# A tenth slot for expert weights, and four units of them asked for earlier, in a two-layer mixer and mixture-of-experts kernel

## The chip, the core and the metric

The kernel runs on one core of a Trainium2 chip. The metric is the device time in microseconds of one execution; the figure given for a kernel is the median of its runs.

## The reference

Two layers over x of 256 tokens by 2048, all float32. Each layer:

```
z   = h @ w_in[l]                       # 2048 x 5648, split into 13 parts
mix = concat(rg_lru(..), short_conv(..), gla(..), local_attention(..)) @ w_out[l]
h   = layer_norm(ALPHA * h + mix)
g   = top-1 of 4 groups of softmax(h @ w_rg + b_rg);  e = top-2 of its 4 experts
ffn = sum over the chosen experts of weight * (silu(h @ w_gate[e]) * (h @ w_up[e])) @ w_down[e]
h   = layer_norm(ALPHA * h + ffn)
```

There are 16 experts per layer; w_gate[e] and w_up[e] are 2048 x 512, w_down[e] is 512 x 2048, so an expert's weights are 12 MB and a layer's 192 MB. All of them are read, once per layer.

## The kernel before

Five engines run hand-ordered streams and meet at semaphores. SyncE issues almost every load, on one queue.

*Projections.* The input projection (11 column blocks of 512) and the output projection (4) are cut into 60 quarters of 1 MB, numbered n. `load_quarter` (L333) puts quarter n into one of six raw buffers (`w_raw(n % 6)`, 8 KiB per partition each, at the start of `room`), and for n of 6 or more waits until TensorE is done with quarter n-6 (`w_used`, L345: at least n - 5). ScalarE rounds a quarter to fp32r (`round_w`, L522 to L527) when TensorE is done with quarter n-4, VectorE subtracts to get the rest (`split_w`, L1143), and TensorE multiplies three times (L815, L818, and L975 in the output projection). Between the quarters stand the pieces of the four mixers: the LRU's product (`lru_done`), the rounding and splitting of the mix (`mix_rounded`, `mix_split`).

*Experts.* An expert's weights are six units of 2 MB: four of gate and up (`unit_gu`), two of down (`unit_down`). They go into nine slots in turn, unit u into slot u % 9, at the places of `SLOT_KIB` in `room`, which the projections used before. Unit u has two DMAs of 1 MB each (L439 for gate and up, L443 for down). In SyncE's loop over the 96 units of a layer, units 0 to 2 follow quarter 59 at once, unit 3 waits for quarter 56 of the output projection (`NQ - 4`), units 4 and 5 for 58, unit 6 for 60; at unit 9 (`u == SLOTS`) SyncE also asks for the norm's gain and shift (L414, L416), and from there unit u waits until the last block of tokens of its slot's former expert has used it: after each quarter of the gate and up product (`gu_quarter`, `gu_done`), after half the down product (`y_half`) or after all of it (`y_done`).

*Order of experts.* The tokens are sorted into blocks of 32 per expert. Experts 0 and 1 always come first (`FIXED = 2`), the others by their number of blocks, most first. Their numbers are in a table that VectorE writes (L1638 and the tensor_tensor after it, `tab_ready`); SyncE waits for it at unit 12, the first of the third expert. Ahead of it in VectorE's order stand the multiply of h by the gain (after `gb1_loaded`), `hidden` of the first block and the second half of that multiply.

*Blocks.* `expert_block` (TensorE) multiplies a block by gate and up (L1080), gathers the next block's rows (L1022), adds the former block's result into h (L1037), transposes (L1089, L1030), and does the down product in two halves (L1098). Experts run in a hardware loop: its body holds three experts, it turns five times, and the sixteenth expert stands behind it. Inside it each expert has a loop over its blocks.

*The next layer.* `load_entry` (L348) asks for quarters 0 and 1 of the next layer when the last block's gate and up product is done (`gu_done`), for 2 to 5 when its down product is (`y_done`). ScalarE rounds quarter 0 ahead of its part of the final layer norm (L750 to L754).

The memory for GpSimd's DMA descriptors has its default size before; GpSimd issues no DMA in this kernel.

Of the kernel before, what the change touches and what calls it, by code (L numbers as in the profile page):

```python
# [15 lines left out]
P = 128  # L16
BLK = 32
KB = 256
# [28 lines left out]
def trunk(nc, x, ln0_g, ln0_b, w_in, conv_a_w, conv_a_b, lru_wa, lru_ba, lru_wx, lru_bx, lru_lam, conv_b_w,  # L47
          gla_wa2, gla_ba2, gla_norm_w, att_rel_bias, w_out, ln1_g, ln1_b, w_rg, b_rg, w_re, b_re,
          w_gate, w_up, w_down, ln2_g, ln2_b, out):
    _, T, D = x.shape  # L50
    L, E = w_gate.shape[0], w_gate.shape[1]
# [11 lines left out]
    NQ = 4 * (N_IN + N_OUT)  # L63
    UNITS = 6
    AHEAD = 3
    SLOTS = 9
    PER_E = 6
    FIXED = 2
    assert NQ % UNITS == 0 and T == 256 and D == 2048 and F == 512
    ALPHA = float((2 * L) ** 0.25)  # L70
    LN_EPS, RMS_EPS = 1e-5, 1e-6
# [3 lines left out]
    with ctx:  # L75
        def sb(name, shape, dt=F32):
            return ctx.enter_context(nc.sbuf_tensor(name, shape, dt))
# [9 lines left out]

        room_at = (nc.sbuf_base + 31) // 32 * 32
        room = sb("room", [P, 184 * KB])
        ring_at, arena_at = room_at, room_at + 96 * 1024  # L90
        SLOT_KIB = (64, 80, 112, 0, 16, 128, 32, 48, 96)

        def part(name, shape, at):

# [131 lines left out]
            return room[:, i * 2048:i * 2048 + 2048].rearrange("p (k n) -> p k n", k=4)  # L226

        def slot_words(u):
            at = SLOT_KIB[u % SLOTS] * KB
            return room[:, at:at + 4096]  # L230

        def unit_gu(u):

            return slot_words(u).rearrange("p (m k n) -> p m k n", m=2, k=4)

        def unit_down(u):

            return slot_words(u).rearrange("p (f n) -> p f n", f=2)
# [72 lines left out]
        def expert_row(eng, row, e):  # L311


            lo, hi = {0: (1, T // BLK), 1: (0, 4096), 2: (0, E - 1), 3: (1, 4096), 4: (E, NB_MAX), 5: (E - 1, 4096)}[row]
            return eng.value_load(tabi[0:1, row, bass.ds(e, 1)], min_val=lo, max_val=hi)
# [17 lines left out]
        def _(eng):  # L333
# [13 lines left out]
            def load_entry(l):  # L347

                if l:
                    last_block = expert_row(eng, 3, E - 1)  # L350
                    eng.wait_ge(gu_done, last_block)
                for n in range(2):
                    load_quarter(l, n)
                if l:
                    eng.wait_ge(y_done, last_block)
                for n in range(2, UNITS):
                    load_quarter(l, n)
                if l == 0:
                    for v in range(2 * L):
                        for m in range(2):  # L360
                            src = ((ln1_g, ln1_b), (ln2_g, ln2_b))[v % 2][m][v // 2]
                            eng.dma_start(lnc[:, v + 1, m, :], src.rearrange("(p k) -> p k", k=KD)).then_inc(lnc_loaded, 16)
                    for m in range(1, L):
                        load_parameters(eng, m)
                eng.wait_ge(pads_ready, l + 1)
                for c in range(4):
                    eng.dma_start(c_wa2[32 * c:32 * c + RANK, :], gla_wa2[l]).then_inc(small_loaded.sem, 16)
                eng.dma_start(c_wca[:, :, 0:RANK], w_in[l, :, C_A:C_A + RANK].rearrange("(p k) n -> p k n", k=KD)
                              ).then_inc(small_loaded.sem, 16)
                load_vectors(*((ln0_g, ln0_b) if l == 0 else (ln2_g[l - 1], ln2_b[l - 1])))  # L370

            def load_vectors(g, b):
                for m, v in enumerate((g, b)):
                    eng.dma_start(gb_in[:, m, :], v.rearrange("(o n) -> o n", o=1).to_broadcast([P, D])
                                  ).then_inc(gb_in_loaded, 16)
# [6 lines left out]
            for l in range(L):  # L382
                for m, w in enumerate((lru_wa, lru_wx)):
                    eng.dma_start(r_w[:, m, :, :], w[l].rearrange("h i j -> i h j")).then_inc(lru_loaded.sem, 16)
                for n in range(UNITS, 18):
                    load_quarter(l, n)
                eng.wait_ge(gsc_done.sem, gsc_done.at(l, 1))
                rb = att_rel_bias[l]
                src = bass.AP(tensor=rb.tensor, offset=rb.offset + P + 1,
                              ap=[[1, P], [att_rel_bias.shape[2], HEADS], [1, T]])  # L390
                eng.dma_start(blocks(a_H, HEADS), src).then_inc(bias_loaded.sem, 16)
                for n in range(18, 40):
                    load_quarter(l, n)
                eng.wait_ge(att_pT.sem, att_pT.at(l, 1))
                eng.dma_start(wr[:, :, 0:G], w_rg[l].rearrange("(p k) g -> p k g", k=KD)).then_inc(router_loaded.sem, 16)
                eng.dma_start(wr[:, :, G:NR], w_re[l].rearrange("(p k) g -> p k g", k=KD)).then_inc(router_loaded.sem, 16)
                eng.dma_start(br[:, 0:G], b_rg[l:l + 1].to_broadcast([P, G])).then_inc(router_loaded.sem, 16)
                eng.dma_start(br[:, G:NR], b_re[l:l + 1].to_broadcast([P, E])).then_inc(router_loaded.sem, 16)
                for n in range(40, NQ):
                    load_quarter(l, n)  # L400

                eng.wait_ge(mix_split.sem, mix_split.at(l, 4))

                def weights(w, e):

                    if e < FIXED:
                        return w[l, e]
                    return w.rearrange("l e a b -> (l e) a b")[bass.ds(l * E + number, 1)].rearrange("o a b -> (o a) b")

                for u in range(PER_E * E):  # L410
                    e, i = u // PER_E, u % PER_E
                    if u == SLOTS:
                        eng.wait_ge(rows_zero.sem, rows_zero.at(l, 1))
                        eng.dma_start(gain_1, ln1_g[l:l + 1].to_broadcast([P, D])).then_inc(gb1_loaded.sem, 16)  # L414

                        eng.dma_start(shift_rows[0:P:BLK, :], ln1_b[l].rearrange("(c n) -> c n", c=4)).then_inc(gb1_loaded.sem, 16)  # L416
                    if e == FIXED and i == 0:
                        eng.wait_ge(tab_ready.sem, tab_ready.at(l, 1))
                    if e >= FIXED and i == 0:
                        number = expert_row(eng, 2, e)  # L420
                    if u >= SLOTS:

                        if u == SLOTS:
                            eng.wait_ge(tab_first.sem, tab_first.at(l, 1))
                        if u == SLOTS or (u - SLOTS) % PER_E == 0:
                            last_block = expert_row(eng, 3, (u - SLOTS) // PER_E)
                        eng.wait_ge((*gu_quarter, gu_done, y_half, y_done)[(u - SLOTS) % PER_E], last_block)
                    elif u == 2:
                        eng.wait_ge(w_used.sem, w_used.at(l, 4 * N_IN))
                    elif u == 3:  # L430
                        eng.wait_ge(w_used.sem, w_used.at(l, NQ - 4))
                    elif u == 4:
                        eng.wait_ge(w_used.sem, w_used.at(l, NQ - 2))
                    elif u == 6:
                        eng.wait_ge(w_used.sem, w_used.at(l, NQ))
                    if i < 4:
                        for m, w in enumerate((w_gate, w_up)):
                            src = weights(w, e).rearrange("(p k) n -> p k n", k=KD)
                            eng.dma_start(unit_gu(u)[:, m], src[:, 4 * i:4 * i + 4, :]).then_inc(unit_loaded[u % SLOTS], 16)  # L439
                    else:  # L440
                        src = weights(w_down, e).rearrange("(k p) n -> p k n", p=P)
                        for f in range(2):
                            eng.dma_start(unit_down(u)[:, f, :], src[:, 2 * (i - 4) + f, :]  # L443
                                          ).then_inc(unit_loaded[u % SLOTS], 16)
                if l + 1 < L:
                    load_entry(l + 1)
                else:
                    eng.wait_ge(y_done, expert_row(eng, 3, E - 1))
                    load_vectors(ln2_g[l], ln2_b[l])
# [313 lines left out]
        def _(eng):  # L763
# [31 lines left out]
            for l in range(L):  # L795
# [270 lines left out]
                def expert_block(g, first_unit, period):  # L1066

                    def loaded(u):
                        per_layer = len(range(u % SLOTS, PER_E * E, SLOTS))
                        eng.wait_ge(unit_loaded[u % SLOTS], period * 64 + 32 * (per_layer * l + u // SLOTS + 1))  # L1070

                    eng.wait_ge(xe_ready, g + 1)
                    for i in range(4):
# [43 lines left out]
                    with eng.Fori(0, n) as j:  # L1117
                        expert_block(g1 + j, first_unit, period)

                with eng.Fori(0, E // 3) as period:  # L1120
                    for i in range(3):
                        expert(period * 3 + i, PER_E * i, period)
                expert(E - 1, PER_E * (E - 1), 0)

                eng.wait_ge(place_ready, g0 + nb + l + 1)
# [583 lines left out]
```

## Time and profile before

| | us |
|---|---|
| median of 3 runs | 1731.58 |
| lowest and highest | 1730.28, 1732.0 |
| span of the profiled execution | 1724.8 |
| TensorE matmul busy | 1563.0 (91%) |
| VectorE busy | 948.2 (55%) |
| ScalarE busy | 545.7 (32%) |
| GpSimd busy | 48.4 (3%) |
| read from memory | 541.96 MB, 315 GB/s over the span |

The times are of whole executions. The profile is one execution on the core, from its first to its last instruction; its page gives the span and no time around it. Busy time of TensorE is modelled at its ends, so a busy TensorE is not one at its peak. DMA share is the mean busy share of the core's 16 DMA engines. The time to landing of a DMA runs from its issue to its completion. Times within the profile are from the span's start.

### The profile page before, as it was taken

The numbers are of one execution on the slowest core, as the hardware profiler recorded it, in microseconds if no ns is written. First come the engines' busy times: TensorE is split into PE (matmuls) and PEld (weight loads), VectorE is DVE, ScalarE is ACT, GpSimd is POOL, SyncE is SP. The second block draws the span as 40 slices with busy tenths as digits, with TensorE's granted clock in tenths as the row PEclk, the third lists the DMA queues.
The fourth block names the chain that finished last, engine by engine and source line by source line (L and its number), as shares of the span: only waits on it lengthen the run. The fifth ranks groups of instructions, "written<-read, shape, count | busy, mean of one in ns | idle before, by whom it ended". The sixth has DMA issues, their size and how long they took to land.

```text
span 1724.8 us, 38658 instructions
## 1 busy us (share of the span) xinstructions
PE 1563.0 (91%) x16272; PEld 1086.2 (63%) x16273; DVE 948.2 (55%) x1544; ACT 545.7 (32%) x694; POOL 48.4 (3%) x36
## 2 busy tenths in 40 slices
PE   8999999997999999866599999999989999986764
PEld 8999899884444444422299999998744444432221
DVE  7657655646566555522476476466466555543235
ACT  4553443423222222111264543533322222211112
POOL 0004000000000000000000040000000000000000
PEclk9999999999999999988899999999989999988787
DMA  8654455579999999999965444555899999999996
GB/s 295 213 173 133 152 170 192 188 288 411 416 422 422 421 422 415 423 422 421 401 229 179 159 143 163 165 191 195 352 406 422 422 422 421 420 422 422 422 422 268
DMA packets 138935, 545.21 MB, mean 316 GB/s; under 512 B 23036, under 2 KB 26336, under 8 KB 88552
## 3 DMA queue, kind: packets, MB, share of 16 engines
q1 hardware_dynamic: 138468, 544.05, 81.0%
q8 instruction: 58, 0.95, 0.2%
q14 instruction: 21, 0.17, 0.0%
q10 hardware_dynamic: 388, 0.04, 0.0%
HBM read 541.96 MB, written 2.10 MB: 315 GB/s over the span
## 4 chain that ended last, share of the span: by engine, by line
PE 74%; SPq 14%; DMA 5%; DVE 3%; issue 2%; DVEq 1%; ACT 0%; ACTq 0%
PE ps L818 24%; PE ps L1080 14%; PE ps L975 10%; SPq L439 9%; PE ps L1098 7%; PE ps L815 5%; SPq L443 5%; PE ps L1022 3%; PE ps L1037 3%; DMA room<-in_w_up_dram 3%; DMA room<-in_ln_b_dram 2%; PE ps L1057 1%; PE ps L1030 1%; PE ps L894 1%; PE ps L1089 1%
## 5 line engine op out<-in xcount | busy, mean ns | idle before, releaser
L1080 PE MATMUL ps<-room 128*32 128x256 f32 x6016 | 377.6, 409 | 101.1 <-DMA room<-in_w_up_dram 90.0
L1143 DVE TENSOR_TENSOR w_lo<-room,w_hi 128x2048 fp32r<-128x2048 f32 (+1 forms) x121 | 280.9, 2331 | 233.3 <-ACT w_hi L527 232.8
L1080 PEld LDWEIGHTS ps<-room 128*32 128x32 f32 x6016 | 202.8, 116 | 290.6 <-DMA room<-in_w_up_dram 111.6
L818 PE MATMUL ps<-hT_hi,w_hi 128*128 128x256 f32 x1152 | 330.7, 287 | 0.9 <-DVE w_lo L1143 0.7
L818 PE MATMUL ps<-hT_hi,w_lo 128*128 128x256 f32 x1152 | 327.5, 284 | 0.0
L818 PE MATMUL ps<-hT_lo,w_hi 128*128 128x256 f32 x1152 | 327.5, 284 | 0.0
L527 ACT ACTIVATE w_hi<-room 128x2048 fp32r<-128x2048 f32 x120 | 228.3, 1914 | 228.4 <-PE ps L818 101.5
L1143 DVE TENSOR_TENSOR h<-h,ps 128x512 f32<-128x512 f32 x376 | 232.9, 682 | 15.3 <-PE ps L1037 15.0
L1143 DVE TENSOR_TENSOR room<-room,ps 128x128 f32<-128x128 f32 (+2 forms) x53 | 18.6, 354 | 392.8 <-ACT room L734 389.3
L818 PEld LDWEIGHTS ps<-hT_hi,w_hi 128*128 128x128 f32 x1152 | 222.8, 193 | 3.8 <-issue 2.4
L818 PEld LDWEIGHTS ps<-hT_hi,w_lo 128*128 128x128 f32 x1152 | 222.7, 193 | 0.7 <-issue 0.5
L818 PEld LDWEIGHTS ps<-hT_lo,w_hi 128*128 128x128 f32 x1152 | 222.7, 193 | 0.0
L1098 PE MATMUL ps<-room 128*32 128x512 f32 x1504 | 184.1, 608 | 9.0 <-DMA room<-in_w_down_dram 8.8
L734 ACT ACTIVATE room<-ps 128x128 f32<-128x128 f32 x47 | 13.1, 278 | 383.8 <-PE ps L1080 383.8
L975 PE MATMUL ps<-w_hi,mix_hi 128*128 128x512 f32 x256 | 100.0, 391 | 0.0
L975 PE MATMUL ps<-w_lo,mix_hi 128*128 128x512 f32 x256 | 99.6, 389 | 0.0
L975 PE MATMUL ps<-w_hi,mix_lo 128*128 128x512 f32 x256 | 99.6, 389 | 0.0
L1022 PE MATMUL ps<-room 128*32 128x512 f32 x784 | 95.8, 606 | 0.0
L1098 PEld LDWEIGHTS ps<-room 128*32 128x32 f32 x1504 | 40.5, 112 | 76.1 <-issue 58.5
L1037 PEld LDWEIGHTS ps<-y_hi,place 32*128 32x128 f32 x392 | 25.1, 183 | 93.1 <-DVE h L1143 47.0
L738 ACT ACTIVATE place<-ps 128x256 fp32r<-128x256 f32 x47 | 18.1, 385 | 178.5 <-PE ps L1062 178.5
L726 ACT ACTIVATE room<-ps 128x512 f32<-128x512 f32 (+1 forms) x96 | 42.4, 441 | 92.3 <-PE ps L1022 73.9
(256 smaller groups left out, 1650.6 us busy)
## 6 DMA issues: line engine op xcount, KB each, us to landing
room<-in_w_gate_dram SPq DMA_DIRECT2D x128, 1024.0 KB, 19.4
room<-in_w_up_dram SPq DMA_DIRECT2D x128, 1024.0 KB, 22.3
room<-in_w_down_dram SPq DMA_DIRECT2D x128, 1024.0 KB, 17.1
room<-in_w_in_dram SPq DMA_DIRECT2D x88, 1024.0 KB, 5.0
room<-in_w_out_dram SPq DMA_DIRECT2D x32, 1024.0 KB, 5.0
room<-in_ln_g_dram SPq DMA_DIRECT2D x5, 1024.0 KB, 6.1
room<-in_ln_b_dram SPq DMA_DIRECT2D x3, 1024.0 KB, 7.3
h<-in_x_dram SPq DMA_DIRECT2D x4, 512.0 KB, 6.4
```

The source lines that it names most:

```text
L439: eng.dma_start(unit_gu(u)[:, m], src[:, 4 * i:4 * i + 4, :]).then_inc(unit_loaded[u % SLOTS], 16)
L443: eng.dma_start(unit_down(u)[:, f, :], src[:, 2 * (i - 4) + f, :]).then_inc(unit_loaded[u % SLOTS], 16)
L527: eng.activation(w_hi[n % 4][:], w_raw(n % UNITS), ACT.Copy).then_inc(w_rounded.sem, 1)
L726: eng.activation(dst, ps[:, b, 0:dst.shape[1]], ACT.Copy).then_inc(ready, 1)
L815: last = eng.matmul(ps[:, b + o, :], x_[:, kk, o * P:o * P + P], w_, start=opens, stop=ends)
L818: last = eng.matmul(ps[:, b + o // 2, (o % 2) * T:(o % 2) * T + T], w_[:, o * P:o * P + P], x_[:, kk, :], start=opens and o % 2 == 0, stop ...
L975: last = eng.matmul(ps[:, b + t, :], m[:, k, t * P:t * P + P], w, start=(q == 0 and k == 0 and j == 0), stop=(q == 3 and k == 3 and j == 2))
L1022: last = eng.matmul(ps[r0:r0 + BLK, 3, :], hot[:, t, :], h_k[:, t, 4 * c:4 * c + 4, :], start=(t == 0), stop=(t == NT - 1), tile_position= ...
L1037: last = eng.matmul(ps[:, bank, :], place[r0:r0 + BLK, t * P:t * P + P], y[r0:r0 + BLK, :], start=(i == 0), stop=(i == 1), tile_position=( ...
L1080: last = eng.matmul(ps[r0:r0 + BLK, 0, 0:2 * P], xe[:, x0:x0 + BLK], unit_gu(u)[:, :, k, c * P:c * P + P], start=(i == 0 and k == 0), stop ...
L1098: last = eng.matmul(ps[r0:r0 + BLK, 2, :], hmT[:, BLK * f:BLK * f + BLK], unit_down(u)[:, f % 2, c * 512:c * 512 + 512], start=(f == 0), s ...
L1143: return eng.tensor_tensor(o, a, b, op)
```

## The change

Ten slots in place of nine. The tenth is a tensor of its own (`spare`, 16 KiB per partition); room for it comes from the memory kept for GpSimd's DMA descriptors, which is set to 1024 bytes per partition. Every slot's old place moves up by one, so that unit u now lies where unit u-1 lay, and unit 0 in `spare`. The body of SyncE's loop becomes `load_unit`. Unit 0 is asked for right after quarter 24, unit 1 after quarter 44 (waiting for the LRU's product), unit 2 after quarter 54 (waiting for the mix's split), unit 3 after quarter 57 (waiting for quarter 44). Units 4, 5 and 6, and 7 take the waits that 3, 4 and 5, and 6 had; from unit 10 on a slot is waited for, and the gain and shift are asked for ahead of unit 10. TensorE's loop over experts holds five of them and turns three times, because 30 units fill ten slots three times. At the start of layer 1, quarters 0 and 1 wait for half the last down product and not for the last gate and up product.

```
-    SLOTS = 9
+    SLOTS = 10
+    AHEAD_OF = {24: 0, 44: 1, 54: 2, 57: 3}
...
+        spare = sb("spare", [P, 16 * KB])
-        SLOT_KIB = (64, 80, 112, 0, 16, 128, 32, 48, 96)
+        SLOT_KIB = (None, 64, 80, 112, 0, 16, 128, 32, 48, 96)
...
         def slot_words(u):
-            at = SLOT_KIB[u % SLOTS] * KB
-            return room[:, at:at + 4096]
+            at = SLOT_KIB[u % SLOTS]
+            return spare[:] if at is None else room[:, at * KB:at * KB + 4096]
...
                 if l:
                     last_block = expert_row(eng, 3, E - 1)
-                    eng.wait_ge(gu_done, last_block)
+                    eng.wait_ge(y_half, last_block)
...
+            def load_unit(l, u):
...
+                elif u == 1:
+                    eng.wait_ge(lru_done.sem, lru_done.at(l, 1))
+                elif u == 2:
+                    eng.wait_ge(mix_split.sem, mix_split.at(l, 4))
+                elif u == 3:
+                    eng.wait_ge(w_used.sem, w_used.at(l, 4 * N_IN))
+                elif u == 4:
+                    eng.wait_ge(w_used.sem, w_used.at(l, NQ - 4))
+                elif u == 5:
+                    eng.wait_ge(w_used.sem, w_used.at(l, NQ - 2))
+                elif u == 7:
+                    eng.wait_ge(w_used.sem, w_used.at(l, NQ))
...
                 for n in range(18, 40):
                     load_quarter(l, n)
+                    if n in AHEAD_OF:
+                        load_unit(l, AHEAD_OF[n])
...
                 for n in range(40, NQ):
                     load_quarter(l, n)
-                eng.wait_ge(mix_split.sem, mix_split.at(l, 4))
...
-                for u in range(PER_E * E):
...
+                    if n in AHEAD_OF:
+                        load_unit(l, AHEAD_OF[n])
+                for u in range(4, PER_E * E):
+                    load_unit(l, u)
...
-                        eng.wait_ge(unit_loaded[u % SLOTS], period * 64 + 32 * (per_layer * l + u // SLOTS + 1))
+                        eng.wait_ge(unit_loaded[u % SLOTS], period * 96 + 32 * (per_layer * l + u // SLOTS + 1))
...
-                with eng.Fori(0, E // 3) as period:
-                    for i in range(3):
-                        expert(period * 3 + i, PER_E * i, period)
+                with eng.Fori(0, E // 5) as period:
+                    for i in range(5):
+                        expert(period * 5 + i, PER_E * i, period)
...
-    nc = _bacc.Bacc("TRN2", target_bir_lowering=False, num_devices=1)
+    nc = _bacc.Bacc("TRN2", target_bir_lowering=False, num_devices=1, dynamic_dma_scratch_size=1024)
```

## Rows read from the trace of the kernel before

**Rows 1.** The page's forty slices: TensorE and DMA busy, in tenths

```profile
PE   8999999997999999866599999999989999986764
...
DMA  8654455579999999999965444555899999999996
```

**Rows 2.** Stretches: us, busy (count) of PE PEld DVE ACT POOL, clock, DMA, GB/s

```profile
436.00:836.00 400.00, 354.77 (x5106) 165.88 (x5098) 195.61 (x441) 80.51 (x156) 0.00 (x0) 0.95 1.01 421
1287.00:1696.00 409.00, 352.07 (x4939) 162.15 (x4933) 186.69 (x422) 77.09 (x150) 0.00 (x0) 0.93 1.01 422
385.00:387.00 2.00, 2.00 (x11) 1.65 (x10) 0.00 (x0) 0.00 (x0) 0.00 (x0) 1.00 0.32 53
```

**Rows 3.** The chain that ended last, near the end of layer 0

```profile
816.77 26.04 DMA room<-in_w_up_dram
```

**Rows 4.** Timeline of SyncE's issues: units 4 and 5, 12, and 12 of layer 1

```profile
385.49 2.13 SPq L443 DMA_DIRECT2D room<-in_w_down_dram  x4
...
427.96 0.35 SPq L439 DMA_DIRECT2D room<-in_w_gate_dram  x1
...
1278.22 0.35 SPq L439 DMA_DIRECT2D room<-in_w_gate_dram  x1
```

**Rows 5.** Timeline of VectorE: the multiply by the gain, and the table

```profile
416.47 2.29 DVE L1143 TENSOR_TENSOR h<-h,room 128x2048 f32<-128x2048 f32 x1 [1.95 <-DMA room<-in_ln_b_dram]
...
427.06 0.16 DVE L1143 TENSOR_TENSOR tabi<-room 128x14 int32<-128x14 f32 x1
```

**Rows 6.** Stretches around the issue of unit 12 and at 685 us

```profile
429.00:435.00 6.00, 5.81 (x52) 3.27 (x56) 5.85 (x12) 0.45 (x2) 0.00 (x0) 0.55 0.92 348
...
685.00:686.00 1.00, 1.00 (x24) 0.65 (x20) 0.00 (x0) 0.00 (x0) 0.00 (x0) 1.00 0.88 270
```

**Rows 7.** Landings, issued at 385.5, 1235.4 to 1236.7, 428.0, 1278.2, 429.4, 452.3

```profile
DMA to landing us min/median/max: 4.9/8.6/12.3
...
DMA to landing us min/median/max: 4.8/7.9/12.4
...
DMA to landing us min/median/max: 7.0/8.0/9.0
...
DMA to landing us min/median/max: 7.3/8.4/9.6
...
DMA to landing us min/median/max: 14.4/14.4/14.4
...
DMA to landing us min/median/max: 23.5/24.9/26.4
```

**Rows 8.** Stretches: a block, the sum of two blocks, the projections of layer 0

```profile
451.94:466.96 15.02, 15.02 (x229) 7.48 (x233) 8.43 (x20) 3.41 (x7) 0.00 (x0) 1.00 1.02 421
...
sum 30.36, PE 30.20 PEld 14.64 DVE 17.62 ACT 7.08 POOL 0.00; mean PE 15.10 PEld 7.32 DVE 8.81 ACT 3.54 POOL 0.00
...
19.50:394.50 375.00, 373.49 (x2559) 344.65 (x2559) 228.17 (x218) 169.61 (x156) 21.52 (x5) 0.99 0.59 198
```

**Rows 9.** ScalarE rounding quarter 58, and a quarter's landing (issued 341.7)

```profile
363.73 1.92 ACT L527 ACTIVATE w_hi<-room 128x2048 fp32r<-128x2048 f32 x1 [3.52 <-PE ps L975]
...
DMA to landing us min/median/max: 5.0/5.0/5.0
```

**Rows 10.** Timeline at the layer's end: TensorE's first down half, ScalarE after rounding

```profile
849.37 1.92 PE L1098 MATMUL ps<-room 128*32 128x512 f32 x16
...
859.82 0.20 ACT L750 ACTIVATE room<-sums 128x4 f32<-128x4 f32 x1 [1.02 <-DVE h L1659]
```

**Rows 11.** Instruction packets, MB, share: 19 to 395, 395 to 470, 470 to 830, 1240 to 1250 us

```profile
q8 instruction: 21, 0.34, 0.4%
...
q8 instruction: 6, 0.10, 0.5%
...
q14 instruction: 4, 0.03, 0.0%
...
q8 instruction: 1, 0.02, 0.6%
```

More of the change, by code:

```diff
@@ L370, in load_entry, with weights @@
                 load_vectors(*((ln0_g, ln0_b) if l == 0 else (ln2_g[l - 1], ln2_b[l - 1])))
+            expert_regs = {}
+            def weights(w, l, e):
+                if e < FIXED:
+                    return w[l, e]
+                return w.rearrange("l e a b -> (l e) a b")[bass.ds(l * E + expert_regs["number"], 1)
+                                                           ].rearrange("o a b -> (o a) b")
+            def load_unit(l, u):
+                e, i = u // PER_E, u % PER_E
+                if u == SLOTS:
+                    eng.wait_ge(rows_zero.sem, rows_zero.at(l, 1))
+                    eng.dma_start(gain_1, ln1_g[l:l + 1].to_broadcast([P, D])).then_inc(gb1_loaded.sem, 16)
+                    eng.dma_start(shift_rows[0:P:BLK, :], ln1_b[l].rearrange("(c n) -> c n", c=4)).then_inc(gb1_loaded.sem, 16)
+                if e == FIXED and i == 0:
+                    eng.wait_ge(tab_ready.sem, tab_ready.at(l, 1))
+                if e >= FIXED and i == 0:
+                    expert_regs["number"] = expert_row(eng, 2, e)
+                if u >= SLOTS:
+                    if u == SLOTS:
+                        eng.wait_ge(tab_first.sem, tab_first.at(l, 1))
+                    if u == SLOTS or (u - SLOTS) % PER_E == 0:
+                        expert_regs["last_block"] = expert_row(eng, 3, (u - SLOTS) // PER_E)
+                    eng.wait_ge((*gu_quarter, gu_done, y_half, y_done)[(u - SLOTS) % PER_E], expert_regs["last_block"])
+                elif u == 1:
[10 more added lines that the diff above has]
+                    eng.wait_ge(w_used.sem, w_used.at(l, NQ))
+                if i < 4:
+                    for m, w in enumerate((w_gate, w_up)):
+                        src = weights(w, l, e).rearrange("(p k) n -> p k n", k=KD)
+                        eng.dma_start(unit_gu(u)[:, m], src[:, 4 * i:4 * i + 4, :]).then_inc(unit_loaded[u % SLOTS], 16)
+                else:
+                    src = weights(w_down, l, e).rearrange("(k p) n -> p k n", p=P)
+                    for f in range(2):
+                        eng.dma_start(unit_down(u)[:, f, :], src[:, 2 * (i - 4) + f, :]
+                                      ).then_inc(unit_loaded[u % SLOTS], 16)
@@ L400, in _ @@
                     load_quarter(l, n)
-                eng.wait_ge(mix_split.sem, mix_split.at(l, 4))
[L404 to L408, printed above, removed]
-                for u in range(PER_E * E):
[L411 to L444, printed above, removed]
```

## The prediction

> **What bounds the kernel now.** I read the page's forty slices first [rows 1]. Both layers look alike: some 390 us in which TensorE is at 9 tenths and the DMA mostly at 4 to 6, then some 460 us in which the DMA stands at 9. The stretches by hand say it sharper [rows 2]: from 436 to 836 us the DMA share is 1.01 and the rate 421 GB/s, in the second layer 1.01 and 422. The chain of waits ends a layer with a landing that took 26.04 us from its issue [rows 3], and gives TensorE most of what lies before. But a chain names only what came last; the DMA had no gap there either. So each expert stage ends when its stream of weights ends. A unit is two transfers of 1024 KB, at 422 GB/s 4.97 us, and 96 units are 477 us.
>
> Only an earlier start of the stream or fewer holes in it can shorten that. So I looked for the latest thing that it waits for. SyncE's issues [rows 4] show it: units 4 and 5 (down) go out at 385.49, then units 6 to 8, the gain of the norm and units 9 to 11, and unit 12 at 427.96. Unit 12 belongs to the third expert, the first whose number comes out of the table, and the table is written at 427.06 [rows 5]. Unit 12's twin in layer 1 goes out at 1278.22. Its slot is no obstacle: before, it is unit 3's, and vector takes that product's result ahead of the table in its own order.
>
> **Where the queue stands at that moment.** At 385 to 387 the queue is empty and moves 53 GB/s [rows 2]; so it starts at 386.9, 1.4 us after the issue. Then it has units 4 to 11 and the gain, 8 x 4.97 + 2.5 = 42.3 us, and is through at 429.2. Unit 12, asked for at 427.96, can move its first bytes at 427.96 + 1.4 = 429.4. The stream of before runs dry just as unit 12 comes: between 429 and 435 the rate is 348 GB/s [rows 6].
>
> **The change, part by part.**
> 1. *Four units asked for early.* Units 0 to 3 come in during the projections; unit 4 goes out where unit 3 did, unit 5 at 385.49, then units 6 to 9 and the gain. Between 385.49 and the gain lie five units both before (4 to 8) and after (5 to 9), so the gain lands where it did, and so starts vector's first multiply with it, which waited 1.95 us for it [rows 5], and all that follows, the table included. The DMA time that is saved turns into idle DMA: ahead of 385, and from 429.2 less unit 9's 4.97, 424.2, to 429.4.
> 2. *What is left of it.* Unit 12 meets an empty queue. Its first transfer landed 7.0 us after its issue, in layer 1 7.3 us; from an empty queue a first transfer took 4.9 and 4.8 us [rows 7]. Gain 2.1 + 2.5 = 4.6 us. The 84 units behind it keep their 4.97 us each.
> 3. *The tenth slot.* A two-block expert keeps TensorE for 30.36 us [rows 8], its six units the queue for 29.8, so the lead shrinks by 0.6 us per such expert; at 685 it is used up and the rate falls to 270 GB/s [rows 6]. One slot more closes this hole of 0.4 us (1 - 270 / 421) and a little beside it. Bounds 0 and 0.6; I take 0, since some engines were not idle.
> 4. *Units between the quarters.* ScalarE rounds a quarter when TensorE frees a buffer; it is 3.52 us idle until then, and not for the DMA [rows 9]. A quarter goes out five before the one that TensorE finishes and is rounded two quarters (2 x 5.44 us) after its issue; it lands 5.0 us after it [rows 9]. That leaves 5.9 us of cover against a unit's 4.97, less the time that the queue is idle between two quarters. Cost 0; without the cover up to 2 us. SyncE's issues of a unit are shorter than its idle time between quarters. The new waits are over when SyncE comes to them: quarter 44 goes out when TensorE is done with 39, and the LRU's product follows split 36; quarter 54 with 49, and the mix's last split stands ahead of split 47; unit 3 waits for 44, long done. So nothing is queued behind them.
> 5. *The end of layer 0.* Quarters 0 and 1 of layer 1 go out after the first half of the last down product, which ends at 851.3, and not when the up products end. Alone in the queue, the first lands some 5.0 us later, at 856.4. ScalarE rounds it in the 1.9 us that end 1.02 us before 859.82 [rows 10], from 856.9. Cost 0, bounds 0 and 1. Quarters 2 to 5 keep their wait. Next to be late would be the layer norm's row sums on ScalarE, queued behind that rounding.
> 6. *Code.* The loop over experts holds five bodies, not three. TensorE has 229 + 233 = 462 records per block [rows 8]. From 19.5 to 394.5 us it ran 2 x 2559 = 5118, and its queue fetched 21 packets of instructions [rows 8, 11], 244 records each. A body is 1.9 packets; three are 5.7, and 6 are fetched between 395 and 470. While the loop turns four more times, none is (the four that are there belong to the other queue) [rows 11]. Five bodies are 9.5 packets, and no row tells whether so many stay. If they do, 4 more are fetched per layer; if none stays, 2 x 9.5 on top in the second and third turn, 23. A packet takes time of one of the 16 DMA engines: with one between 1240 and 1250 [rows 11], the fourth transfer of units 4 and 5, issued last at 1236.7, landed 12.4 us later, at 1249.1 [rows 7]; 4.8 us from 1235.4 and three times 2.48 give 1247.7. So 1.4 us late, as a transfer is complete when all its engines are. In turn over 16 engines, 23 packets cost 23 x 1.4 / 16 = 2.0 us per layer, 4 packets 0.4. That they take turns: the transfer issued at 429.4 landed 14.4 us later, at 443.8, the one issued at 452.3 26.4 us later, at 478.7 [rows 7]: 34.9 us for seven units, where 7 x 4.97 = 34.8, in spite of three packets. Bounds 0.4 and 2.0 per layer if in turn. I take 2.0: 9.5 packets are nearer to straight code, which fetches each, than to the 5.7 that stayed. TensorE's own stall at the jump back is hidden, since the DMA sets the end.
>
> The Trainium skill, "Runtime: NRT & Kernel Launch", section "Instruction fetch mechanics", gives TensorE an instruction memory of 128 KiB, 2048 instructions, filled in blocks of 16 KiB, and says that a branch out of its window forces a fetch. By its figure five bodies (2310 records) don't fit and three (1386) do; for three the trace agrees, for five no run here shows it yet.
>
> Sum: -4.6 + 2 x 2.0 = -0.6 us. The profiled span is 1724.8 us and the page has no time around it; the median of the runs, 1731.58, is 6.8 us above it (runs 1730.28 to 1732.0). 1731.6 - 0.6 = **1731.0 us**.
>
> **The rivals.**
> - *The code stays in* (0.30): -4.6 + 0.8 = -3.8, 1727.8 us. For it: three bodies stay. Against: five are 1.7 times as long.
> - *The stream gains a whole unit or more* (0.08), if the queue was deeper at 428 than I count or the table comes earlier. One unit per layer, 9.9 us: 1721.7; all four, 39.8: 1691.8. Against: SyncE's wait for the table [rows 4, 5].
> - *Slower: the packets pile up on few DMA engines* (0.10). 23 packets over 4 engines are 8.1 us per layer: 1731.6 - 4.6 + 16.2 = 1743.2. It decides from (3.5 + 4.6) / 2 / 1.4 = 2.9 packets more on the slowest engine per layer. For it: few packets could be followed; against: three of them cost the slowest engine nothing.
> - The forecast itself has 0.52: 1728 to 1735, with points 4 and 5 at their bounds.
>
> **How the numbers follow.** A measurement of this kernel tells about 0.2%, 3.5 us, from no change: faster is below 1728.1, slower above 1735.0. The forecast gives 0.06 faster, 0.42 same, 0.04 slower; code that stays 0.19 and 0.11; the unit 0.08 faster; the pile 0.10 slower. Together 0.33, 0.53, 0.14. The range 1725.5 to 1736.0 leaves out the unit and the pile, 0.18.
>
> **What would show it.** Right: unit 12 issued at 428 and 1278 as now, an idle DMA for 3 to 5 us before; its first transfer landing in 4.9 us; no hole at 685; some 104 instruction packets in place of 58, all through the first half of the expert stage and beyond. Wrong: the gain landing earlier or unit 12 issued earlier; 66 packets (the code stays); ScalarE waiting for quarters in the projections; the layer's last unit landing later than now; vector's first split of layer 1 late.

## The result, and the profile after

The changed kernel takes **1741.17 us** (median; lowest 1736.08) against 1732.0 for the kernel before beside it. The ratio is 1.0048, with an interval of 1.0035 to 1.0061: slower by 8.3 us, where 1731.0 was predicted and a range that ended at 1736.0. One of its seven runs took 2557.22 us at a mean granted clock of 0.554 where the others had 0.947 to 0.956; it counts in this median, without it 1740.5, and is left out of the ratio. Differences below are ratios times 1731.6 us. The profiled execution took 1739.34 us, 1.8 more than its span. Counted so, the profiled execution of before took some 1726.6, 5 below its median: so a difference of a few us between two profiled executions says little, and I compare stalls and rates inside them.

The page of the changed kernel: share of TensorE and of the DMA by slice, rate, instruction packets, and the group of matmuls on the new slot.

```profile
span 1737.5 us, 38642 instructions
PE   8999999997997999786699999999989989987664
DMA  8554556759999899999975554567599999999996
GB/s 307 198 182 171 169 168 224 242 212 375 421 421 420 357 417 416 416 420 420 374 243 180 170 186 161 168 241 276 224 373 421 420 402 415 416 414 420 421 420 271
q8 instruction: 114, 1.87, 0.4%
L1094 PE MATMUL ps<-spare,room 128*32 128x256 f32 x640 | 48.5, 444 | 52.5 <-issue 37.9
```

Against [rows 1] two slices stand out in the middle of the stretches that were full: 357 GB/s in the slice that begins at 564.7 us, and 402 at 1390. No landing, slot or engine is named beside the idle time of the last group: TensorE stood still 37.9 us for "issue", that is for nothing the profile shows. The timeline of TensorE (start, duration, instruction, in brackets the idle time before it and what ended that) finds four stalls, all on the first matmuls of `spare` after a jump:

```profile
553.72 3.64 PE L1094 MATMUL ps<-spare,room 128*32 128x256 f32 x32 [11.26 <-issue]
...
719.72 3.31 PE L1094 MATMUL ps<-spare,room 128*32 128x256 f32 x32 [11.45 <-issue]
...
1408.77 3.53 PE L1094 MATMUL ps<-spare,room 128*32 128x256 f32 x28 [6.60 <-issue]
...
1555.99 3.31 PE L1094 MATMUL ps<-spare,room 128*32 128x256 f32 x28 [7.33 <-issue]
```

They are the four jumps back of the loop over experts, from the fifth to the sixth and from the tenth to the eleventh of each layer. Their sum is 36.6 us. Before, the longest time for which a matmul of this product waited for "issue" was 0.8 us. The clock falls with each stall too. In the table of stretches (its columns are named below) the granted clock, the number behind the busy times, is 0.50 just after the first stall, the lower of its two levels, and 1.00 again from 559 us:

```profile
553.70:557.00 3.30, 3.28 (x32) 1.63 (x36) 0.00 (x0) 0.00 (x0) 0.00 (x0) 0.50 1.01 422
559.00:562.00 3.00, 3.00 (x60) 1.71 (x56) 0.00 (x0) 0.00 (x0) 0.00 (x0) 1.00 1.01 421
```

So the 32 matmuls behind the stall take 3.64 us in place of 1.94 (e1 below, at the same place), which is 1.7 us more of TensorE's time beyond the idle time.

What the stall does to the stream is in SyncE's timeline at the first jump (start, duration of the issues), in the DMA view from 540 to 575 us (40 slices of 0.875 us), and in a table of stretches (busy times of the engines, clock, DMA share, GB/s):

```profile
544.00 3.00 SPq L416 DMA_DIRECT2D room<-in_w_up_dram  x1
573.16 0.85 SPq L420 DMA_DIRECT2D spare<-in_w_down_dram  x2
```

```profile
GB/s 440 431 412 431 393 431 421 421 421 421 393 440 421 403 421 431 403 440 431 421 384 412 431 431 412 431 403 431 421 412 412 356 243 140 112 28 0 0 9 140
q8 instruction: 4, 0.07, 0.8%
room<-in_w_up_dram SPq DMA_DIRECT2D x2, 1024.0 KB, 27.0
```

```profile
430.00:565.00 135.00, 122.97 (x1804) 58.60 (x1802) 68.13 (x155) 27.67 (x54) 0.00 (x0) 0.93 1.01 421
565.00:585.00 20.00, 20.00 (x306) 9.68 (x310) 13.49 (x30) 4.71 (x10) 0.00 (x0) 1.00 0.75 299
585.00:650.00 65.00, 64.20 (x976) 30.97 (x972) 38.62 (x88) 16.42 (x32) 0.00 (x0) 1.00 1.00 413
650.00:700.00 50.00, 49.76 (x777) 24.86 (x773) 26.56 (x60) 10.70 (x21) 0.00 (x0) 1.00 1.00 413
700.00:730.00 30.00, 18.55 (x253) 7.97 (x249) 9.93 (x25) 3.84 (x8) 0.00 (x0) 0.83 1.01 421
730.00:760.00 30.00, 27.81 (x428) 13.50 (x431) 16.63 (x37) 6.86 (x13) 0.00 (x0) 1.00 1.01 420
```

A TensorE that stands still frees no slot, so SyncE has nothing to issue between 544.00 and 573.16. The queue had 27 us of work. It keeps 421 GB/s until 567 us, is empty at 571.5, and moves next to nothing until the issue at 573.16: (421 - 299) / 421 x 20 = 5.8 us lost. After that the slots are used up and the stream goes at TensorE's pace, 413 GB/s, which is six units (12.58 MB) in the 30.36 us of [rows 8]: another 8 / 421 x 115 = 2.2 us until 700. Together 8.0 us from the first jump of layer 0. The second one, at 708, costs the stream nothing that these rows show: behind it stand experts of one block, and TensorE catches up before the queue is empty. Layer 1 has its first stall at 1402 us:

```profile
1410.00:1450.00 40.00, 39.23 (x590) 19.25 (x586) 18.18 (x42) 7.41 (x15) 0.00 (x0) 0.97 0.98 401
1450.00:1560.00 110.00, 101.16 (x1495) 47.90 (x1487) 61.49 (x139) 24.70 (x48) 0.00 (x0) 0.97 1.01 414
```

The same count gives 1.9 + 1.8 = 3.7 us there, 11.7 us in both layers. The times below put the jumps at 7.8 us, give or take 3; what of the difference is this one execution, and what is taken back elsewhere, is open.

### The profile page after: what moved, and what is told of

It is laid out like the page before. It is cut to its first block, busy times and chain, and to the rows that moved or that the text cites. A ratio compares the mean times of both kernels' runs of the same rounds, so it can differ in the third digit from the quotient of the medians.

```text
span 1737.5 us, 38642 instructions
## 1 busy us (share of the span) xinstructions
PE 1558.7 (90%) x16272; PEld 1087.1 (63%) x16273; DVE 948.9 (55%) x1544; ACT 545.7 (31%) x694; POOL 48.4 (3%) x36
## 4 chain that ended last, share of the span: by engine, by line
PE 75%; SPq 12%; DMA 5%; DVE 3%; issue 3%; DVEq 1%; ACT 0%; ACTq 0%
PE ps L832 24%; PE ps L1094 14%; PE ps L989 10%; SPq L416 8%; PE ps L1112 8%; PE ps L829 5%; PE ps L1036 4%; SPq L420 3%; PE ps L1051 3%; DMA room<-in_w_up_dram 3%; DMA room<-in_ln_b_dram 2%; PE ps L1071 1%; PE ps L1044 1%; PE ps L958 1%; PE ps L1103 1%
## 5 line engine op out<-in xcount | busy, mean ns | idle before, releaser
L1094 PE MATMUL ps<-room 128*32 128x256 f32 x5376 | 329.3, 401 | 67.0 <-DMA room<-in_w_up_dram 62.6
L1094 PEld LDWEIGHTS ps<-room 128*32 128x32 f32 x5376 | 179.5, 115 | 227.2 <-DMA room<-in_w_up_dram 82.1
L1112 PE MATMUL ps<-room 128*32 128x512 f32 x1376 | 168.0, 607 | 8.3 <-DMA room<-in_w_down_dram 8.1
L1036 PE MATMUL ps<-room 128*32 128x512 f32 x784 | 96.7, 608 | 0.0
L1094 PE MATMUL ps<-spare,room 128*32 128x256 f32 x640 | 48.5, 444 | 52.5 <-issue 37.9
L1112 PEld LDWEIGHTS ps<-room 128*32 128x32 f32 x1376 | 37.0, 112 | 68.5 <-issue 53.6
```

The costliest lines, as they stand in the source:

```text
L1036: last = eng.matmul(ps[r0:r0 + BLK, 3, :], hot[:, t, :], h_k[:, t, 4 * c:4 * c + 4, :], start=(t == 0), stop=(t == NT - 1), tile_position= ...
L1094: last = eng.matmul(ps[r0:r0 + BLK, 0, 0:2 * P], xe[:, x0:x0 + BLK], unit_gu(u)[:, :, k, c * P:c * P + P], start=(i == 0 and k == 0), stop ...
L1112: last = eng.matmul(ps[r0:r0 + BLK, 2, :], hmT[:, BLK * f:BLK * f + BLK], unit_down(u)[:, f % 2, c * 512:c * 512 + 512], start=(f == 0), s ...
```

## The experiments

Two theories at first. *Jump*: the body of five experts doesn't stay in TensorE's instruction memory, each jump back waits for code, and that stall runs through the slots into the stream. Its rival: the *slots* (their places, the tenth, the early units) or the added *packets* alone cost the time. In the table every kernel beside its before; the last column is the ratio in us.

| run | us | before | ratio | us by ratio | packets |
|---|---|---|---|---|---|
| changed kernel | 1741.17 | 1732.0 | 1.0048 [1.0035, 1.0061] | +8.3 | 114 |
| e1_straight | 1731.72 | 1731.23 | 1.0003 [0.9990, 1.0017] | +0.5 | 103 |
| e2_before_straight | 1736.97 | 1731.23 | 1.0030 [1.0012, 1.0049] | +5.2 | 103 |
| e3_first_apart | 1725.95 | 1731.23 | 0.9978 [0.9962, 0.9994] | -3.8 | 58 |
| e4_slots_only | 1741.14 | 1731.23 | 1.0069 [1.0044, 1.0094] | +11.9 | 114 |
| e5_early_only | 1731.3 | 1733.86 | 0.9992 [0.9976, 1.0008] | -1.4 | 58 |
| e6_before_body6 | 1746.76 | 1733.86 | 1.0092 [1.0060, 1.0125] | +15.9 | 108 |
| e8_eight_slots | 1800.13 | 1733.86 | 1.0389 [1.0370, 1.0408] | +67.4 | 118 |
| e9_first_apart_three_known | 1724.15 | 1731.49 | 0.9954 [0.9938, 0.9971] | -8.0 | 58 |
| e10_before_three_known | 1728.82 | 1731.49 | 0.9989 [0.9973, 1.0004] | -1.9 | 58 |
| e11_two_turns | 1736.03 | 1728.38 | 1.0032 [1.0016, 1.0048] | +5.5 | 107 |
| e12_both_gates | 1720.7 | 1728.38 | 0.9938 [0.9913, 0.9962] | -10.7 | 69 |

**e1_straight: the changed kernel without the loop over experts.**

```
-                with eng.Fori(0, E // 5) as period:
-                    for i in range(5):
-                        expert(period * 5 + i, PER_E * i, period)
-                expert(E - 1, PER_E * (E - 1), 0)
+                for e in range(E):
+                    expert(e, PER_E * e, 0)
```

> The changed kernel with its loop over experts written out, sixteen bodies one behind the other and no jump back over five bodies. Theory J (what was lost is the time that TensorE stands at the two jumps back of each layer, 7 to 13 us each, because the code there has to be fetched again, and the slots that it holds meanwhile): no stall of more than 2 us between experts, no hole in the stream, some 30 packets of instructions per expert stage and so about 120 in all, and 1731 us (1729 to 1734): 1732.0 - 4.6 for the earlier unit 12 + 2 x 22 packets x 1.4 / 16. Theory P (the packets themselves take the DMA engines' time): as many packets or more than the changed kernel's 114, so 1741 us or above.

The stalls are gone and the rate is full where it was 299 and 413. Timeline of TensorE at the same place, and two of the stretches:

```profile
541.95 1.90 PE L1112 MATMUL ps<-room 128*32 128x512 f32 x16
543.91 1.94 PE L1094 MATMUL ps<-spare,room 128*32 128x256 f32 x32
```

```profile
565.00:585.00 20.00, 19.94 (x286) 10.12 (x282) 11.58 (x29) 4.72 (x10) 0.00 (x0) 1.00 1.01 420
585.00:650.00 65.00, 64.96 (x992) 32.75 (x988) 39.88 (x88) 14.82 (x31) 0.00 (x0) 1.00 1.01 421
```

Same slots, same early units, 103 packets in place of 114, and 7.8 us less (by the two intervals give or take 3). The jumps, with the 11 packets that they fetch anew, cost what separates the two.

**e2_before_straight: the kernel before, written out in the same way** (nine slots, no early units).

> The kernel before with its loop over experts written out: the code is fetched once per expert, nothing else changes. Theory J: packets alone, 2 x 22 x 1.4 / 16 = 3.9 us at most, 1732 to 1736 us, no stall. Theory P: the loss of the changed kernel and more, 1741 to 1746 us.

45 packets more and no stall: +5.2 us (+2.1 to +8.5), 2.6 per layer. The prediction took 2.0 for 23 packets. In the DMA views from 440 to 830 us and from 1290 to 1690 us the queue of the weights moved 163.53 and 167.78 MB here, 164.13 and 168.50 before, and 46 instruction packets more came in the two stretches. So the weights came 1.32 MB, or 3.1 us, later in this execution; the rest of the 5.2 us, if it is real, wasn't located.

**e3_first_apart: the tenth slot without the longer body.** `spare` holds unit 0 of each layer alone, the other 95 go round nine slots, and so the body stays at three experts.

```
+    RING = 9
...
+        def slot(u):
+            return 1 + (u - 1) % RING if u else 0
...
-                with eng.Fori(0, E // 5) as period:
-                    for i in range(5):
-                        expert(period * 5 + i, PER_E * i, period)
-                expert(E - 1, PER_E * (E - 1), 0)
+                expert(0, 0, 0)
+                with eng.Fori(0, E // 3) as period:
+                    for i in range(3):
+                        expert(period * 3 + i + 1, PER_E * (i + 1), period)
```

> The changed kernel with short code: the spare slot serves unit 0 alone, units 1 to 95 go round the nine others, so expert 0 stands in front and a loop of three bodies turns five times. The early asks are as in the change. Both theories: 58 packets, no stall at the jump back, unit 12 lands 2 to 3 us after an empty queue as in the change, and 1727 to 1729 us (1732.0 - 4.6, with up to 0.8 for the lost tenth slot). If the early asks themselves cost something, in the projections or at the layer's end, it is 1732 us or above.

58 packets as before, no stall, and 3.8 us faster than before: what the early units and the empty queue at unit 12 give is there once the code fits. Its stretch that answers to [rows 2]:

```profile
436.00:836.00 400.00, 355.19 (x5110) 165.71 (x5106) 195.48 (x441) 80.47 (x156) 0.00 (x0) 0.95 1.01 421
```

So the +8.3 us are -3.8 (e3), +4.3 for the packets (e1 less e3, which differ in the tenth slot's place in the ring too), and +7.8 for the jumps (changed kernel less e1). Each of the two differences is good to some 3 us.

**e4_slots_only: ten slots and five bodies, no early units** (`AHEAD_OF` empty, units 0 to 3 after quarter 59).

> The changed kernel without the early asks: ten slots and five bodies, all units asked for behind quarter 59. Both theories: the same stalls at the jumps and the same 114 packets, so 1741 us within 2; since unit 12 waits for the table, asking for four units early is worth 0 to 1 us. If the early asks were what costs, it would be 1732 us or less.

Stalls of 11.05, 11.15, 6.52 and 7.43 us again: they need no early units. By the medians the early units gain nothing on top of this kernel, by the ratios 3.6 us, with intervals that overlap.

**e5_early_only: nine slots, three bodies, units 0 to 2 asked for early.**

> The kernel before (nine slots, three bodies) with units 0 to 2 asked for early, behind quarters 44, 54 and 57. By the sum of the prediction the gain of the norm and units 9 to 11 still fill the queue until 429, so unit 12 comes no sooner: 1732 us within 1.5. If the time that the DMA saves comes back, 3 x 4.97 us per layer, it is near 1702.

-1.4 us, with 1 inside the interval. Units 0 to 2 come in early and the DMA idles more between 374 and 385 us instead, but the fourth early unit is missing: units 4 to 11 stand ahead of unit 12 as before, and the queue still has work at 424 (stretches of this kernel):

```profile
374.00:385.00 11.00, 11.00 (x50) 9.11 (x49) 4.07 (x8) 0.20 (x1) 0.00 (x0) 1.00 0.16 66
424.00:430.00 6.00, 1.80 (x15) 0.69 (x8) 5.48 (x15) 0.00 (x0) 0.00 (x0) 0.95 0.97 408
```

**e6_before_body6: the kernel before with a body of six**, turning twice, and four experts behind it; one jump back per layer.

```
-                with eng.Fori(0, E // 3) as period:
-                    for i in range(3):
-                        expert(period * 3 + i, PER_E * i, period)
-                expert(E - 1, PER_E * (E - 1), 0)
+                with eng.Fori(0, 2) as period:
+                    for i in range(6):
+                        expert(period * 6 + i, PER_E * i, period)
+                for e in range(12, E):
+                    expert(e, PER_E * e, 0)
```

> The kernel before with a loop of six bodies that turns twice and four bodies behind it: one jump back per layer, from expert 5 to expert 6, over 11 packets of code; slots and asks as before. Theory J: one stall of 7 to 12 us on TensorE per layer, inside the stretch where its lead over the stream is down to 1 or 2 us, so the stream stands for 5 to 9 us per layer: 1742 to 1750 us. Theory P: about 110 packets, 1736 to 1741 us, without a stall that matters.

Two stalls, 10.78 us at 574.5 and 6.64 at 1435.3, and +15.9 us; less e2's 5.2 for its packets, 10.7 us for 17.4 us of stall. The changes to the slots aren't needed for the loss: the length of the body alone makes it.

**e7_quiet_queue: the changed kernel with little in the queue.** From unit 24 on only 64 numbers of each row are loaded, so most weights of experts 4 to 15 are left out and its time is no measure.

> The changed kernel, where units 24 to 95 of each layer load only 64 numbers per row and matrix in place of whole rows (the experts from the fifth on compute with what lies in the slots). So the DMA is nearly idle at both jumps back. If TensorE's wait for code is long because its packets stand behind the weights in the DMA engines, the stall falls from 7 to 11 us to 2 or 3 us. If it is the fetch itself that is slow, it stays at 6 us or above.

Timeline of TensorE at the second jump of layer 0:

```profile
712.97 3.64 PE L1096 MATMUL ps<-spare,room 128*32 128x256 f32 x32 [5.89 <-issue]
```

5.94, 5.89, 4.39 and 4.58 us for the four jumps, in place of 11.26, 11.45, 6.60 and 7.33. Neither theory's number: in layer 0 about half of a stall is there without the weights in the way, and about half goes with them. It is one execution. The times of the packets agree. In the changed kernel the first two after the jump start at 544.7 and 550.6, 5.9 us apart, and TensorE goes on at 553.72; here they start at 546.9 and 550.4, 3.5 apart. At the first jump of layer 1, where the stall is shorter, TensorE goes on before the second has come (1404.3, 1410.4, and the matmul at 1408.77); at the second jump two come 1.0 us apart (1549.8, 1550.8, and the matmul at 1555.99). Why the layers differ is open.

**e8_eight_slots: the kernel before with eight slots and a body of four**, turning four times: 4 x 462 = 1848 records of TensorE, 7.6 packets.

> The kernel before with eight slots and a loop of four bodies that turns four times: 4 x 1.9 = 7.6 packets of code, between the 5.7 that stayed and the 9.5 that did not. If TensorE keeps eight packets, there is no stall and about 58 packets in all, and the slot less costs the stream: the lead is one unit shorter, so holes of up to 5 us per layer, 1735 to 1742 us. If it keeps fewer than 7.6, there are some 28 packets per layer and stalls of 7 to 11 us at three jumps per layer, 1750 us or more.

Six stalls at its six jumps, 10.78, 11.83, 10.80, 11.59, 11.45 and 11.59 us, together 68.0, and a loss of 67.4, of which some 5 for packets as in e2. Timeline of TensorE at the first two, and the rate from 530 to 560 us:

```profile
528.98 3.64 PE L1080 MATMUL ps<-room 128*32 128x256 f32 x32 [10.78 <-issue]
...
664.42 4.07 PE L1080 MATMUL ps<-room 128*32 128x256 f32 x36 [11.83 <-issue]
```

```profile
GB/s 415 448 426 393 415 415 426 415 448 404 350 240 229 55 44 0 0 0 0 0 0 0 0 0 0 120 208 415 393 459 404 448 426 448 426 415 426 404 448 404
```

The queue is all but empty for ten slices of 0.75 us. So four bodies aren't kept either, and with fewer slots most of each stall is lost. What of the 67.4 us the missing slot takes without a jump wasn't measured apart.

**e9 and e10: the third expert's number without the table.** Unit 12 waits for the table because only two experts are fixed. `FIXED = 3` takes this wait away from e3's kernel (e9) and from the kernel before (e10).

> The kernel of e3 (early asks, spare slot for unit 0 alone, three bodies) with expert 2 as a third fixed expert, so that units 12 to 17 can be asked for without the table (one small addition on VectorE more, for the third row of the table's first part). If the wait for the table is what keeps the early asks from paying, the queue does not run dry between 424 and 430 us and the stream keeps what the projections loaded for it: up to 5 us per layer below e3, so 1716 to 1721 us. If something else sets the start of the stream (free slots, or TensorE's blocks), it stays within 2 us of e3.

> The kernel before with the third fixed expert alone. Its queue holds units 9 to 11 until 429 us, so not waiting for the table saves only the dip behind it, 1 to 2.5 us per layer: 0 to 5 us below the kernel before. If the table was worth more than that without early asks, the account of the queue at 428 us is wrong.

e9 gains 4.2 us more than e3 by the ratios, 1.8 by the medians, less than the first of the two cases expected and within 2 us of e3 by the medians, as in the second; e10 gains 1.9, with 1 inside the interval. The stretch and SyncE's timeline of e9 say why:

```profile
416.00:421.00 5.00, 5.00 (x80) 2.89 (x76) 4.26 (x11) 0.00 (x0) 0.00 (x0) 0.80 0.13 28
```

```profile
419.41 2.58 SPq L424 DMA_DIRECT2D room<-in_w_down_dram  x4
```

The queue is empty from 416 to 421: units 10 and 11 go out at 419.41, when the first block has used their slots. Behind the wait for the number stands the wait for a free slot.

**e11_two_turns: one jump per layer in the changed kernel**, from the fifth expert to the sixth; the other six experts are written out behind the loop.

> The changed kernel, but the loop of five bodies turns twice and six bodies stand behind it in a row: one jump back per layer, from expert 4 to expert 5, in the stretch of two-block experts; the jump from expert 9 to 10 is gone. If the first jump carries the loss, because TensorE is what the slots wait for there, and the second (11.5 and 7.3 us in the changed kernel's trace) is hidden by one-block experts that wait for the stream anyway, the time is that of the changed kernel, 1740 to 1742 us. If both carry half, 1736 to 1737.

Stalls of 10.90 at 544.0 and 6.53 at 1401.1, and +5.5 us. Less e1's +0.5, the first jumps cost 5.0 us, and the changed kernel's second ones 2.8 on top; the medians alone, 1736.03 between 1731.72 and 1741.17, would make it half and half. The intervals don't settle the share. In layer 0 the trace does, for this one execution: the stretches from 565 to 585, 650 and 700 us run at

```profile
565.00:585.00 20.00, 20.00 (x278) 9.11 (x274) 13.04 (x31) 4.60 (x10) 0.00 (x0) 1.00 0.72 291
585.00:650.00 65.00, 64.19 (x988) 30.80 (x985) 39.28 (x89) 15.76 (x32) 0.00 (x0) 1.00 1.00 413
650.00:700.00 50.00, 49.76 (x776) 24.80 (x771) 27.34 (x62) 11.64 (x22) 0.00 (x0) 1.00 1.01 413
```

which is the changed kernel's loss, without the second jump. Where the second jump costs something, if it does, is open.

**e12_both_gates: what the runs point to.** Unit 10 goes into `spare` after unit 0, so it waits for the first use of the first block and not for the slot of unit 1; the ring of nine holds units 1 to 9 and 11 to 94, unit 95 is in `spare` again; three fixed experts; six quarters of the next layer after the fifteenth expert; a body of three that turns four times, with two experts ahead and two behind.

```
+        def slot(u):
+            if u in (0, SLOTS, PER_E * E - 1):
+                return 0
+            return u if u < SLOTS else 1 + (u - 2) % RING
...
+                expert(0, 0, 0)
+                expert(1, PER_E, 0)
+                with eng.Fori(0, 4) as period:
+                    for i in range(3):
+                        expert(period * 3 + i + 2, PER_E * (i + 2), period)
+                expert(E - 2, PER_E * (E - 2), 0)
+                expert(E - 1, PER_E * (E - 1), 0)
```

> The kernel of e9 with the second gate moved too. In e9 the queue is empty from 416 to 421 us because unit 10 waits for the slot of unit 1. Here unit 10 takes the spare slot that unit 0 leaves first, units 11 to 94 go round the nine others, and unit 95 takes the spare one again, so that the next layer's first six quarters can follow when expert 14 is done. Experts 0 and 1 stand in front of a loop of three bodies that turns four times, 14 and 15 behind it: no code is fetched twice. If free slots were the second gate, the stream has no gap from unit 5 to its end and 4 to 5 us per layer come back: 1714 to 1718 us. If not, within 2 us of e9's 1724.

1720.7 us, 10.7 below before by the ratio: the fastest of all, though its interval overlaps e9's, and 2.7 above the upper end of what was expected. Its stretches from 411 to 436, from 414 to 421 and from 436 to 836 us:

```profile
411.00:436.00 25.00, 20.14 (x217) 9.22 (x213) 19.59 (x50) 3.03 (x5) 0.00 (x0) 0.84 0.73 296
414.00:421.00 7.00, 5.35 (x64) 2.74 (x68) 5.47 (x18) 1.32 (x2) 0.00 (x0) 0.76 0.17 26
436.00:836.00 400.00, 359.32 (x5142) 167.26 (x5134) 197.88 (x448) 80.91 (x158) 0.00 (x0) 0.94 1.01 421
```

Unit 10 still waits for the first block, and the queue is all but empty for these 7 us. That may be what is missing; no run took it away. An eleventh slot, or a first block that starts earlier, would be next; neither was tried.

## Why the prediction was wrong

Its steps by number.

1. *Early units*: right. The idle DMA moved where it was said to: 374 to 385 us and 424 to 430 us of the changed kernel against 326 and 421 GB/s before in the same stretches. The multiply by the gain started at 415.75 and the table was written at 426.34; [rows 5] have 416.47 and 427.06, and the wait for the gain 1.95 where it is now 1.79.

```profile
374.00:385.00 11.00, 11.00 (x51) 9.10 (x50) 3.65 (x8) 0.20 (x1) 0.00 (x0) 1.00 0.11 45
424.00:430.00 6.00, 1.80 (x9) 1.12 (x6) 5.48 (x15) 0.00 (x0) 0.00 (x0) 0.92 0.41 131
```

2. *Unit 12*: right. It was issued at 427.24 into an empty queue and its first transfer landed 4.7 us later (4.9 predicted; in layer 1 4.8). SyncE's timeline, and the landing of the transfer issued at 427.24:

```profile
427.24 0.35 SPq L416 DMA_DIRECT2D room<-in_w_gate_dram  x1
427.69 0.38 SPq L416 DMA_DIRECT2D room<-in_w_up_dram  x1
```

```profile
DMA to landing us min/median/max: 4.7/4.7/4.7
```

The term was -4.6 us; e3, which has it with nothing that takes it back, is at -3.8 (-6.6 to -1.0).

3. *The tenth slot*: the hole at 685 can't be seen apart from the 413 GB/s of TensorE's pace there. e3 has no tenth slot in its ring and still 421 over the 400 us.
4. *Between the quarters*: cost nothing that shows; e3 carries it and is faster.
5. *The end of layer 0*: nearly as predicted. ScalarE's rounding now waited for its quarter, 0.35 us, and was done before vector's result came. Timeline of ScalarE, which answers to [rows 10]:

```profile
865.27 1.91 ACT L541 ACTIVATE w_hi<-room 128x2048 fp32r<-128x2048 f32 x1 [0.35 <-DMA room<-in_w_in_dram]
867.76 0.20 ACT L764 ACTIVATE room<-sums 128x4 f32<-128x4 f32 x1 [0.57 <-DVE h L1673]
```

6. *Code*: that the five bodies don't stay was right, and the packets nearly so. 23 more per layer were predicted, 22.5 came with the straight kernels and 28 with the jumps, two or three more at each. The term was 4.0 us, and the runs have 5.2 (e2) and 4.3 (e1 less e3), inside their intervals.

**The step that failed is the last sentence of step 6**, "TensorE's own stall at the jump back is hidden, since the DMA sets the end". I named the right event and gave it no length. It is 6.6 to 11.5 us, and the cover that I relied on is the backlog of SyncE's queue, 27 us, which refills only when TensorE frees slots. With experts of two blocks TensorE takes 30.36 us and the queue 29.8 for six units, by my own step 3: there is nothing to catch up with. The stall therefore empties the queue, and the stream goes at TensorE's pace until the experts have one block. The next slot comes free a stall and a block after the last, 11.3 + 15.0 = 26.3 us, with the slower matmuls at the lower clock 28.0 (29.2 between the two issues above), against a backlog of 26.04 us [rows 3]: no cover was left. The right form of step 6 is 4.0 + 7.8; with -4.6 and 1731.6 that is 1738.8, against the 1739.9 that the ratio gives. None of the rivals was it. The one for slower, packets that pile up on few engines, had the right sign and with 1743.2 us the nearest number, but by luck: it asks 16.2 us for the packets, and e1 and e2 have nearly all of them for 4.3 and 5.2.

The Trainium skill, "Runtime: NRT & Kernel Launch", section "Instruction fetch mechanics", says besides what I cited that execution can't continue before the target page of such a branch is there, an "ifetch stall". The traces agree in kind, with 4.4 to 11.8 us for one. The Trainium skill speaks there of a window of two pages; here the 5.7 packets of three bodies stayed, and the measurement decides. I had read this for its count of packets and not for the stall. For the size that the Trainium skill gives, eight blocks of 256 instructions, the runs put the limit no higher and perhaps lower: three bodies of 5.7 packets stay, four of 7.6 (e8) do not. The Trainium skill also says that kernels prefer full unrolling for this reason; here the three kept bodies are 5.2 us faster than the loop written out (e2).

## What to carry to other kernels

Count the records of a hardware loop's body on each engine before making it longer: here a body of three experts stayed in TensorE's instruction memory and turned without a fetch or a stall, and bodies of four, five and six cost a stall at every jump back and a stream of packets beside. If a ring of buffers forces a longer body, take the odd buffers out of the ring (the first unit in a slot of its own) and keep the body. And "hidden, since the DMA sets the end" holds only while the queue's backlog is longer than the stall plus the time to the next free slot; here TensorE and the stream were within 2% of each other for experts of two blocks, and a stall on the engine that looked like the faster one was paid.

## What was unexpected of the hardware

- A jump back to code that isn't kept stalls TensorE by 10.8 to 11.8 us with the weights' queue full, by 6.5 to 7.4 in layer 1 of the kernels with nine and ten slots (e8's layer 1 has the full 11.5), and by 4.4 to 5.9 with a quiet queue. In layer 0 it is two 16 KiB packets one after the other, 5.7 to 6.0 us apart among weights (once 7.0, in e8) and 3.4 to 3.6 without.
- After a stall the granted clock is low, 0.50 and 0.57 over the 3.3 us behind the first two of the changed kernel, and the first 28 to 32 matmuls take 3.3 to 3.6 us in place of 1.9, so each stall costs some 1.5 us beyond its idle time.
- How much of a stall is paid depends on the slots: less e2's 5.2 us for packets, with eight some 62 us for 68.0 us of stall; with nine (e6) 10.7 for 17.4; with ten, 7.8 for 36.6. These include different places in the layer, so they are no law.
- 45 packets of 16 KiB, 0.74 MB of 544, cost a stream bound by the DMA more than their bytes, which would be 1.8 us at 421 GB/s: by the times 5.2 us (2.1 to 8.5), by the bytes of weights in e2's two stretches 3.1 us.
